# The low halves of the experts' down matrices are made by GpSimd instead of VectorE

## The reference

```
scores = sigmoid(t @ w_router);  each token picks 8 of 64 experts (4 of 8 groups), gates w
act    = silu(t @ w_eg[e]) * (t @ w_eu[e])        # w_eg, w_eu: 1024 x 256
routed = sum over the 8 picked e of  w[t, e] * (act @ w_ed[e])   # w_ed: 256 x 1024
out    = x + g2 * (routed + shared expert)
```

## Time and profile before

| | us |
|---|---|
| median of 3 runs | 1826.3 |
| lowest, highest | 1824.06, 1830.0 |
| the profiled execution: its own time | 1813.22 |
| the profiled execution: span of the trace | 1811.3 |
| mean granted TensorE clock in it | 0.948 of full speed |

### The profile page before, as it was taken

One profiled execution on the slowest core, in us unless ns is written; L12 is line 12 of the kernel. 1 busy time (PEld: TensorE's weight loads), 2 busy tenths in 40 slices (PEclk: granted clock), 3 DMA queues, 4 the chain that ended last, 5 costly groups with the idle time before them and its releaser, 6 DMA issues.

```text
span 1811.3 us, 22786 instructions
## 1 busy us (share of the span) xinstructions
PE 1567.9 (87%) x7266; PEld 1222.8 (68%) x7267; DVE 1311.6 (72%) x1672; ACT 935.7 (52%) x1152; POOL 294.3 (16%) x280
## 2 busy tenths in 40 slices
PE   6899889899898998999996679999998899999950
PEld 1676666687677676677775467877776678777730
DVE  2695856466775867867757677888886658888849
ACT  2335536433333243342522367888785658888830
POOL 2000000000100201002002522222223222222210
PEclk9899999999999999999997889999998999999975
DMA  8121121164333233221523379999997759999948
GB/s 289 49 92 66 48 74 47 62 210 159 110 100 117 73 100 118 94 70 47 196 92 117 114 255 342 372 373 359 365 368 287 268 217 376 366 350 356 360 163 360
DMA packets 108834, 361.43 MB, mean 200 GB/s; under 512 B 19932, under 2 KB 30368, under 8 KB 81856
## 3 DMA queue, kind: packets, MB, share of 16 engines
q1 hardware_dynamic: 81120, 295.20, 44.5%
q0 software_dynamic: 22688, 45.29, 6.7%
q10 hardware_dynamic: 4928, 19.78, 2.7%
HBM read 352.18 MB, written 43.66 MB: 219 GB/s over the span
## 4 chain that ended last, share of the span: by engine, by line
PE 56%; DVE 17%; DMA 15%; ACT 6%; issue 5%; ACTq 1%; SPq 0%; DVEq 0%; POOL 0%; POOLq 0%
PE psum L1493 15%; PE psum L1495 15%; PE psum L1494 14%; DMA rawm<-in_w_exp_up 8%; DMA rawm<-in_w_exp_down 4%; DVE ring L1029 2%; PE psum L859 2%; DVE ofin L1111 2%; DVE cv L2051 1%; ACT ring L951 1%; PE psum L1687 1%; PE psum L1740 1%; ACT hl L1275 1%; PE psum L1647 1%; DVE hl L1826 1%
## 5 line engine op out<-in xcount | busy, mean ns | idle before, releaser
L1029 DVE TENSOR_TENSOR ring<-rawm,ring 128x2048 fp32r<-128x2048 f32 x189 | 429.3, 2287 | 46.4 <-ACT ring L951 45.8
L951 ACT ACTIVATE ring<-rawm 128x2048 fp32r<-128x2048 f32 x189 | 362.4, 1918 | 83.7 <-DMA rawm<-in_w_exp_down 42.5
L1493 PE MATMUL psum<-ring,xT 128*128 128x512 f32 x528 | 223.1, 422 | 25.2 <-DVE ring L1029 20.3
L1826 DVE TENSOR_TENSOR hl<-raw,hl 128x2048 fp32r<-128x2048 f32 x59 | 135.0, 2292 | 113.3 <-ACT hl L1275 112.6
L1495 PE MATMUL psum<-ring,xT 128*128 128x512 f32 x528 | 210.8, 399 | 0.0
L1494 PE MATMUL psum<-ring,xT 128*128 128x512 f32 x528 | 210.0, 398 | 0.0
L1493 PE MATMUL psum<-hl,hT 128*128 128x512 f32 x416 | 170.5, 410 | 6.3 <-DVE hT L2131 3.5
L804 POOL DMA_INDIRECT y_rows<-yb,row_of x64 | 98.8, 1543 | 447.6 <-ACT yb L993 427.3
L1494 PE MATMUL psum<-hl,hT 128*128 128x512 f32 x416 | 164.9, 396 | 0.0
L1495 PE MATMUL psum<-hl,hT 128*128 128x512 f32 x416 | 164.8, 396 | 0.0
L1493 PEld LDWEIGHTS psum<-ring,xT 128*128 128x128 f32 x528 | 101.8, 193 | 52.5 <-DVE ring L1029 18.9
(11 more groups left out here) (374 smaller groups left out, 2945.4 us busy)
## 6 DMA issues: line engine op xcount, KB each, us to landing
rawm<-in_w_exp_down SPq DMA_DIRECT2D x64, 1024.0 KB, 9.6
rawm<-in_w_exp_gate SPq DMA_DIRECT2D x64, 1024.0 KB, 12.0
rawm<-in_w_exp_up SPq DMA_DIRECT2D x64, 1024.0 KB, 14.9
raw<-in_w_in SPq DMA_DIRECT2D x36, 1024.0 KB, 5.1
modraw<-in_w_ada SPq DMA_DIRECT2D x64, 256.0 KB, 2.9
ysum<-y_rows ACTq DMA_DIRECT2D x16, 1024.0 KB, 9.0
raw<-in_w_ada SPq DMA_DIRECT2D x8, 1024.0 KB, 10.1
raw<-in_w_branch_b SPq DMA_DIRECT2D x8, 1024.0 KB, 5.4
```

Source lines behind the costliest of these rows:

```text
L951: A(ring[:, slot, 1, :], rawm[slot][:], ACT.Copy).then_inc(S["m_hi2"], 1)
L1029: TT(ring[:, slot, 0, :], rawm[slot][:], ring[:, slot, 1, :].bitcast(F32), ALU.subtract).then_inc(S["m_lo2"], 1)
L1493: M(dst, lhs(0), rhs(0), start=first, stop=False)
L1826: TT(hl[:, slot, 0, :], raw[slot][:], hl[:, slot, 1, :].bitcast(F32), ALU.subtract).then_inc(S["lo_done"], 1)
```

## The change

Three things move. On DVE, the low half of down e+1 goes out of each turn, and the low half of down 0 out of the start. On POOL, a new `low_down` does the same subtraction with the same operands: for expert 0 behind the first three gathers, and then for expert e+1 at the end of each of POOL's turns, behind the scatter. A new semaphore `m_down` counts these; PE waits for it where it waited for the third of `m_lo2`, which now counts two a turn. To have the semaphore, the router weights' load shares one with an earlier load.

```
+            def low_down(e):
+                slot = SLOT[e % 3][2]
+                if e:
+                    pool.wait_ge(S["m_hi2"], 3 * e)
+                else:
+                    pool.wait_ge(S["hi_done"], len(units) - len(early) + 3)
+                nc.gpsimd.tensor_tensor(ring[:, slot, 0, :], rawm[slot][:], ring[:, slot, 1, :].bitcast(F32),
+                                        ALU.subtract).then_inc(S["m_down"], 1)
             for e in range(3):
                 gather(e)
+            low_down(0)
...
                 if e:
                     pool.wait_ge(S["y_ev"], e)
                     scatter(e - 1)
+                if e + 1 < NE:
+                    low_down(e + 1)
...
                 if whole:
-                    pe.wait_ge(S["m_lo2"], 3 if isinstance(e, int) and e == 0 else e * 3 + 2)
+                    pe.wait_ge(S["m_lo2"], e * 2 + 2)
...
                     pe.wait_ge(S["at_lo"], e)
-                    pe.wait_ge(S["m_lo2"], e * 3)
+                    pe.wait_ge(S["m_down"], e)
...
-                        pe.wait_ge(S["m_lo2"], e * 3 + 3)
+                        pe.wait_ge(S["m_lo2"], e * 2 + 2)
+                        pe.wait_ge(S["m_down"], e + 1)
...
-            for n in range(3):
+            for n in (1, 2):
                 first_lo(n)
...
-                if more_:
-                    split(nxt, e + 1, [2])
...
-                    pool.dma_start(wr[:], w_router[0].rearrange("(p k) n -> p k n", p=P)).then_inc(S["wr_in"], 16)
+                    pool.dma_start(wr[:], w_router[0].rearrange("(p k) n -> p k n", p=P)).then_inc(S["ga_in"], 16)
...
-                    a.wait_ge(S["wr_in"], 16)
+                    a.wait_ge(S["ga_in"], 48)
```

More of the change, by code:

```diff
@@ L569, in build @@
             "g_in", "spilled", "ga_in", "x2_in", "merged", "gate_ready", "m_hi", "m_lo")
-        sem("h2_row", "h2T_ps", "h2T_hi", "h2T_lo", "h2_out", "wr_in", "lg_ps", "lg_ev",
+        sem("h2_row", "h2T_ps", "h2T_hi", "h2T_lo", "h2_out", "m_down", "lg_ps", "lg_ev",
             "sel_ready", "pos_ps", "addr_ready", "table_far", "table_set", "table_in", "tok_ready",
```

## The result

| | before | after |
|---|---|---|
| median, us | 1826.9 (4 runs) | 1865.12 (4 runs) |
| lowest, highest | 1824.06, 1830.0 | 1861.8, 1868.08 |
| profiled execution: own time, span | 1813.22, 1811.3 | 1868.08, 1866.3 |
| first to last transposes of the expert loop | 673.24 | 713.68 |

The ratio of after to before is 1.0218, with a 95% interval of 1.0198 to 1.0237: 38 us slower. A second comparison, on another chip, gave 1.0228 (1.0201 to 1.0256), with before at 1824.76 and after at 1866.29 us.

The account below looks back on a forecast made before the run. PE's own turn of 9.33 us plus late transfers bounded the kernel; POOL's lock on DVE would lengthen turns to 10.58 us, adding 12.5, 19.8 and 4, together +36 us on 1826.3: 1862 us, range 1838 to 1888.

Parts of the forecast that it names:

- its start, from T with the wait in: POOL's subtraction, behind its scatter: starts T + 1.82, T being the start of PE's 24 matmuls, with PE's wait of 1.25 us.
- DVE's low half of up done: DVE's second low half in a turn, held up by POOL: done at T + 11.82 less PE's wait of 1.25 us.
- 25 and 26 turns, cost: Two stretches of the expert loop: turns of 10.58 us instead of 10.08 and 9.82 cost 12.5 and 19.8 us.
- the large experts and single turns: Two experts with over 128 tokens, about 1 us each, and two single turns, 1.2 each: together 4 us.
- DVE's relief: DVE gives up 2.29 us a turn; its low halves wait for ACT and transfers, so no gain was booked.
- The lock: While POOL runs on SBUF operands, a DVE instruction with two SBUF inputs stands still; a turn becomes 10.58 us.
- POOL's duration: POOL's subtraction of the down matrix's low half, alone: 4.4 us, between 3.6 and 5.3.
- the first to start wins: Where POOL and DVE instructions on SBUF operands meet, the earlier runs on; POOL comes first by 1.5 us every turn.
- the clock falls: Rival, 4%: PE's pause of 1.25 us each turn lowers its granted clock to 0.92; +41 us at most, 1903.
- The start: Ahead of the loop, POOL's subtraction for expert 0 is paid from DVE's idle time and saved 2.29 us: nothing gained or lost.
- The gather comes last: Rival, 9%: the next gather, delayed behind POOL's subtraction, lands too late for PE; slower still, 1868 or 1891 us.

Follow-up runs that it names:

- one fill: Against the changed kernel, POOL's subtraction replaced by one fill of the same place, down's low half left out: 1810.57 us, ratio 0.9967 to the kernel before.
- three eighths of the columns: Against the changed kernel, POOL subtracts only columns 1280 to 2047 at the same place, DVE the first 1280: 1807.43 us, ratio 0.9970 to the kernel before.
- one program: Against the changed kernel, POOL's subtraction moved behind the next gather, ahead of the second body: 1885.73 us, ratio 1.0341 to the kernel before.

## Why the prediction was right, and which terms were off

The forecast was 1862 us (1838 to 1888), and 1865 was measured. The mechanism held step by step; that the sum came so close is partly luck, as the large experts cost 15 us more than booked and the regular turns 7 us less. Loop times below are means of two profiles of each kernel.

| step | predicted | measured |
|---|---|---|
| POOL's subtraction | 4.4 us (3.6 to 5.3) | 4.65 |
| its start, from T with the wait in | T + 1.82 | T + 1.23 |
| DVE's low half of up done | T + 10.57 | T + 10.27 |
| turn | 10.58 us | 10.46 and 10.45 in the two stretches |
| DVE's mean for the pair | 3.0 us | 3.22 |
| PE's wait for DVE's low halves | some 70 us | 53.8 us |
| 25 and 26 turns, cost | +32 us | +11 and +14 (25 and 24 turns) |
| the large experts and single turns | +4 us | +19 |
| DVE's relief | 0 | worth about 6 us where nothing takes it back |

- **The lock** was the term that decided, and it held in size too. POOL's end at T + 5.90 and the predicted 2.15 + 2.20 us behind it give T + 10.25; the trace has T + 10.27. Fills of the same length at the same place cost DVE nothing, so it is not POOL being busy. The Trainium skill (SBUF — State Buffer, § Who interferes with whom) says that a DVE instruction with two SBUF inputs contends with a GpSimd instruction that reads SBUF, not with one that only writes it: both halves agree here, 3219 against 2285 ns.
- **POOL's duration** I bounded from smaller multiplications, with the value 0.25 us low. The 4497 ns of the Trainium skill (GPSIMD Engine Reference, § 3.1 Elementwise) was nearer; the measured median is 4652. (The advice that the prediction takes from that skill's SBUF page stands there in § Summary: rules for kernel authors, not in § Who interferes with whom.)
- **POOL's start** was 0.6 us too late, because I gave its scatter the old mean of 1.54 us. In the new phase the scatter runs where DVE has nothing of this kind and takes 1.00. With the duration too short by 0.25 the end was put 0.32 us too late, of which the wait takes half: hence a turn only 0.12 us too long.
- **The large experts** are the mis-sized term: 1 us each was predicted. In POOL's turn the second body holds scatter and subtraction back, and then they come in a row. The timeline behind the first one, and between 1441 and 1449 us the single durations of DVE's pair (ns, min/median/max):

```profile
1441.23 0.97 POOL L804 DMA_INDIRECT y_rows<-yb,row_of  x1 [5.19 <-issue]
...
1441.68 9.53 DVE L1043 TENSOR_TENSOR ring<-rawm,ring 128x2048 fp32r<-128x2048 f32 x2
...
1442.22 4.63 POOL L842 TENSOR_TENSOR ring<-rawm,ring 128x2048 fp32r<-128x2048 f32 x1
...
1451.26 0.80 PE L1505 MATMUL psum<-ring,xT 128*128 128x512 f32 x1 [4.03 <-DVE ring L1043]
```

```profile
L1043 DVE TENSOR_TENSOR ring<-rawm,ring x2: 2279/4801/7323, 1441.7 to 1448.9; 128x2048 fp32r<-128x2048 f32 x2
```

DVE's low half of gate starts 0.54 us ahead of POOL's subtraction and is held by it all the same: it takes 7.32 us and ends 2.16 us behind POOL's end. So the prediction's "the first to start wins" is wrong where the two start this close, and that is what makes the collision here so dear. DVE's pair takes 9.53 us, PE stands 4.03 us, and then its clock falls. Of the windows:

```profile
1440.00:1451.00 11.00, 7.24 (x37) 5.80 (x36) 9.66 (x3) 8.40 (x7) 9.29 (x4) 0.96 0.71 267
1451.00:1463.00 12.00, 11.74 (x44) 9.52 (x45) 6.83 (x7) 4.83 (x5) 8.92 (x5) 0.75 0.76 277
```

Granted 0.75 of full speed in the second window, where the kernel before has 1.00 in the turn of the earlier trace rows. So that turn takes 16.25 us where it was 9.33: 4 from the wait, most of the rest from the clock. The rival "the clock falls" came true, but at two turns and not in all: at pauses of 0.8 us a turn the granted clock stays 1.00. Counted with the turns next to them, the two places cost 8 us each, and the stretch between them 2.6 more.
- **The cost of the regular turns** was too high, 32 instead of 25: the turn 0.12 us too long, over 51 turns where 49 were regular.
- **The start** costs nothing, as said: shown by the loop starts. DVE's and POOL's instructions do collide there (one of DVE's small ones, started 0.18 us ahead of POOL's subtraction, takes 5.26 us where its like takes 0.69), but in DVE's slack.
- **The gather comes last** did not happen in the changed kernel, though the gather instruction grew from a mean of 1125 ns to 2769: a wait of PE for xg is not among its waits. It is what costs in the kernels where the collision is taken away (22.3, 18.6 and 12.5 us of waits for xg), so the slack there was real and thin.
- **DVE's relief**, booked at nothing, is not nothing: one fill gives 0.9967, three eighths of the columns 0.9970. In which turns those 6 us lie was not shown; single profiles of one kernel differ by 5 us in their loop (673.24 and 668.53 us before).

By medians of one chip the change costs 38 and 41.5 us, by the loops 713.6 - 670.9 = 42.7: the table's 44 less 1.7 that the first eight turns gain. That 2048 columns cost this and 768 gain 5 goes with one number, in the turns shown: POOL's end lies 1.83 us behind the moment when DVE takes up its pair (T + 5.90 against T + 4.07), or 0.32.

## What to carry to other kernels

Before work goes to POOL, ask of each of its instructions whether it reads SBUF, and lay it against the timeline of every DVE instruction with two SBUF inputs; the price is the time from DVE's due start to POOL's end, not POOL's busy share. Size the piece to the gap (here 768 of 2048 columns), and then place everything that stands behind it in POOL's queue anew, since each free place is free only while the rest stays where it was. Don't count on DVE being half a microsecond ahead. Work out the rare turns apart: those at two experts of 64 carried over a third of the cost (16 of 43 us), and behind the pause there the granted clock fell too.

## What the runs showed of the hardware

- **POOL's indirect transfers are held by DVE as well.** A gather issued inside DVE's low half of gate takes 2.90 us (1312.57 in the turn above), one issued clear of it 1.00. It ends 0.9 us behind the end of that low half, and DVE is not lengthened by it (2294 ns at most before, with gathers and scatters inside, and some of its low halves starting inside a transfer). So the hold goes one way.
- **DVE holds POOL's subtraction only if it starts clearly ahead.** Over all kernels with the subtraction, DVE's low half started 0.94 to 1.01 us ahead of it 18 times, and each time POOL's was the longer one. Started 0.15 to 0.68 us ahead, 17 times, DVE's was the one held to behind POOL's end. Twice it started 0.05 us ahead and was not held, so the recorded starts alone don't decide, and why stays open.
- **The order sustains itself**: one program ran 25 turns with POOL first at 11.20 us each, and later, from 1515 to 1622 us, eleven turns of 9.75 us on average in which DVE mostly came first.
- **Sizes on POOL**: subtraction of 128x2048 in 4.65 us, 128x1024 in 2.44, 128x768 in 1.92; fill of 128x2048 in 1.83 us (median 1833 ns of 64). The subtraction is thus about 2.2 ns an element and a small constant, against 1.12 on DVE.
